# The expert layer in two passes: one rounded matmul per token for the gate spread, first products of all 128 tiles before any second product

## The chip, the cores and the metric

The kernel runs on one core of one Trainium2 chip. The metric is the time of one execution on the device, in microseconds (us). The engines are TensorE (PE; PEld is its loading of weights), VectorE (DVE), ScalarE (ACT), GpSimd (POOL) and SyncE (SP), which here only issues DMAs.

## The reference, cut to what matters

The program is a block of three layers on 256 tokens of width 1024: two attention layers, a mixer with memory attention, and at the end a layer of experts (PEER). Only the expert layer changes:

```python
def _peer(h, w_query, sub_keys, expert_u, expert_v):
    ...
    g = jax.nn.softmax(top_s, axis=-1).astype(h.dtype)
    ...
    def block(args):
        xt, it, gt = args
        u = expert_u[it]
        act = jax.nn.gelu(jnp.einsum('td,tkd->tk', xt, u))
        return jnp.einsum('tk,tkd->td', gt * act, expert_v[it])
```

There are 128 x 128 = 16384 experts. Each token picks 128 (8 heads, 16 each) by two indices of 0 to 127 and has a gate for each pick. The kernel does it densely: gelu(h u) is made for all experts in 128 tiles of 128 experts, multiplied by a matrix W of gates (zero where a token did not pick the expert), and multiplied by v. The output is the residual plus that, normalised.

## The kernel before, in words

**Precision.** A product of float32 factors is made of three matmuls in the rounded type fp32r: each factor is split into a rounded part (hi, made by ACT as a copy into `whi`, `ghi`) and a remainder (lo, made by DVE or POOL by a subtraction into `wlo`, `glo`); hi x hi, hi x lo and lo x hi are summed. So a tile of u or v (128 partitions x 1024 columns, 512 KB) passes through: a DMA into `raw` or `xw`, ACT's copy, the subtraction, then PE.

**First product** of a tile: 8 steps of 128 along the width. Into a bank of 256 tokens go 16 matmuls of 256 columns with hi weights (`hThi`, `hTlo`) and 8 with lo weights. ACT then applies gelu. **Second product** of a tile: for 2 halves of tokens and 2 halves of the output 3 matmuls of 512 columns each, 12 in all; they accumulate over all tiles in banks 0 to 3, which no other work can use from then on.

**W.** For each token one matmul of two one-hot matrices (rows: its 128 picks; `first_hot` scaled by the gates, `second_hot`) gives its 128 x 128 slice of W. It is a full float32 matmul of 128 columns. DVE makes the one-hots for groups of 8 tokens (L2505, two instructions of 1024 columns), POOL (L1373) and ACT (L1732) multiply by the gates, PE does 8 matmuls per group (`w_group`, L1250, two records each in the trace), ACT copies them from PSUM into the arena, four tokens at a time (L1724).

**Order.** (1) NA = 48 tiles have only their first product early (`early_product`, lines 702 and 705), while DVE picks the experts; after gelu their activations go to DRAM (`spill`, L609). The 32 groups of W stand in pairs behind tiles 29 to 44. (2) The first product of two further tiles and their second, as the hand-over. (3) A loop in rounds of six tiles (`expert_loop`, 78 tiles in all): first product of tile j in a wide form (8 matmuls of 512 columns, L1321, that take hThi and hTlo side by side, and 8 of 256, L1324; ACT and DVE add the halves by L1770 and L2523), then second product of tile j - 2 (L1297). Each load brings u and v together, 1024 KB. (4) The tail: second products of the 48 early tiles. SP issues for tile i the 512 KB of v (L648) and right behind it the 128 KB of activations (L652) into one of 32 places of the arena, with at most four on the way; DVE multiplies them by W (`weigh_again`, L2569), ACT rounds (L1822), DVE subtracts (L2581).

Each engine and the SP queue take their instructions in the written order; semaphores (`wait_ge`) tie them together.

Of the kernel before, what the change touches and what calls it, by code (L numbers as in the profile page):

```python
# [29 lines left out]
XRING = 3  # L30
XBODY = 6
NL = 2 + XBODY * 13
NA = N_KEYS - NL
E_AT = (12, 23)
ACT_GATES = 1
SEL0_AT = 19
SEL1_AT = 27
G0 = 29
GROUPS_W = T // 8
G1 = G0 + GROUPS_W // 2  # L40
HEAD = [(NA + 2 * tile + part, tile, part) for tile in range(2) for part in range(2)]
RAW_OF = [i % 4 if i < G0 - 5 else i % 3 for i in range(NA)] + [0, 1, 2, 0]
SPLIT_OF = [i % 4 if i < G0 - 5 else i % 3 for i in range(NA)] + [0, 1, 2, 3]
LAST_OF_FOUR = G0 - 6


def before(ring, i):

    earlier = [j for j in range(i) if ring[j] == ring[i]]
    return earlier[-1] if earlier else None  # L50


def groups_at(i):

    return range(2 * (i - G0), 2 * (i - G0) + 2) if G0 <= i < G1 else range(0)
# [66 lines left out]
def build(nc, x_d, mem_d, keep_d, tab_d, sml_d, frt_d, final_d, w_d, sk_d, ex_d, out_d):  # L122
    ctx = ExitStack()
    with ctx:
# [53 lines left out]
        def fr(name):  # L178
# [46 lines left out]
        uhi_ready, ulo_ready, vhi_ready, vlo_ready, ghi_ready, glo_ready = (  # L225
            sem(n) for n in ("uhi_ready", "ulo_ready", "vhi_ready", "vlo_ready", "ghi_ready", "glo_ready"))
        iota_ready = sem("iota_ready")
        hotA, hotB, hotC, x_kept = sem("hotA"), sem("hotB"), sem("hotC"), sem("x_kept")
        ex_loaded = [sem(f"ex_loaded{i}") for i in range(XRING)]

# [25 lines left out]
        head_half = sem("head_half")  # L256
        hot_ready, wt_done, wt_taken = sem("hot_ready"), sem("wt_done"), sem("wt_taken")
        aex_loaded = [sem(f"aex_loaded{i}") for i in range(4)]
        auhi_ready, aulo_ready, aa_done, aa_gelu = (sem(n) for n in ("auhi_ready", "aulo_ready", "aa_done", "aa_gelu"))
        act_stored = [sem(f"act_stored{i}") for i in range(3)]  # L260
        act_back = [sem(f"act_back{i}") for i in range(4)]
        b_taken, sum_ready = sem("b_taken"), sem("sum_ready")
        a_done, a_gelu, g_ready, v_done = sem("a_done"), sem("a_gelu"), sem("g_ready"), sem("v_done")
# [152 lines left out]
        iota_ps = bank[4][:, 0:P]  # L416
        wbank = bank[6:8]
# [126 lines left out]
        head_bank = [bank[5 + (NA + n - G1) % 3] for n in range(2)]  # L544
        head_first = [q for q in HEAD if q[2] == 0]

        def early_bank(i):

            return bank[6 + i % 2] if i < G0 else bank[5] if i <= G1 else bank[5 + (i - G1) % 3]

        def ex_slot(i):

            return (i - 2) % XRING

        def ex_uses(i):

            return (i - 2) // XRING + 1

        vslots = [w for i in range(4) for w in [(i % 2, D if i >= 2 else 0)]]

        def v_at(i):

            b, at = (i % 2, D) if i < NL else vslots[(i - NL) % 4]
            return b, slice(at, at + D)

        act_again = [arena[:, 14 * T + T * (m % 32):14 * T + T * (m % 32) + T] for m in range(NA)]
# [3 lines left out]
        def _(sp_):  # L570
# [35 lines left out]

            def store_act(i):
                sp_.wait_ge(aa_gelu, i + 1)
                sp_.dma_start(spill[i], staged[i % 3]).then_inc(act_stored[i % 3], 16)  # L609

            for i in range(NA + 4):
                if i < 2:
                    sp_.wait_ge(lo_ready, len(SPLIT_UNITS) - 3)
                elif i < 4:
                    sp_.wait_ge(lo_ready, len(SPLIT_UNITS) - 2)
                else:
                    sp_.wait_ge(aulo_ready, before(RAW_OF, i) + 1)
                if i < NA:
                    rows_of_u = ex_d[NL + i][:, 0:D]
                else:  # L620
                    _, tile, part = HEAD[i - NA]
                    rows_of_u = ex_d[tile][:, D * part:D * part + D]
                sp_.dma_start(aslots[RAW_OF[i]], rows_of_u).then_inc(aex_loaded[RAW_OF[i]], 16)
                if i >= 6:
                    store_act(i - 6)
            for i in range(NA - 2, NA):
                store_act(i)

            for i in range(2, 2 + XRING):
                sp_.wait_ge(aulo_ready, NA + 3 if i == 2 else NA + 4)  # L630
                sp_.wait_ge(wt_done, T // 4)
# [2099 lines left out]
```

## Time and profile before

| | us |
|---|---|
| three runs, median (lowest, highest) | 1509.1 (1508.21, 1510.73) |
| the profiled execution | 1509.89 |
| its span, first to last instruction | 1508.1 |
| PE busy in the span | 1470.0 |
| DVE, ACT, POOL busy | 889.2, 819.0, 576.4 |

Of the profiled execution's time 1.8 us lie outside its span. Busy shares are means over stages with different limits, so they are read stage by stage below.

### The profile page before, as it was taken

The numbers are of one execution on the slowest core, as the hardware profiler recorded it, in microseconds if no ns is written. First come the engines' busy times: TensorE is split into PE (matmuls) and PEld (weight loads), VectorE is DVE, ScalarE is ACT, GpSimd is POOL, SyncE is SP. The second block draws the span as 40 slices with busy tenths as digits, with TensorE's granted clock in tenths as the row PEclk, the third lists the DMA queues.
The fourth block names the chain that finished last, engine by engine and source line by source line (L and its number), as shares of the span: only waits on it lengthen the run. The fifth ranks groups of instructions, "written<-read, shape, count | busy, mean of one in ns | idle before, by whom it ended". The sixth has DMA issues, their size and how long they took to land.

```text
span 1508.1 us, 24377 instructions
## 1 busy us (share of the span) xinstructions
PE 1470.0 (97%) x8923; PEld 1302.1 (86%) x8923; DVE 889.2 (59%) x2185; ACT 819.0 (54%) x1483; POOL 576.4 (38%) x200
## 2 busy tenths in 40 slices
PE   7999999999999999989999999999999999999998
PEld 6788888788889898889999998888888888887886
DVE  4935259388336431225996662666666666667776
ACT  5556454488456644443556664555555555555554
POOL 6881665700467477456888884000000000000000
PEclk9999999999999999999999999999999999999999
DMA  8740435600334335333665334555555555556774
GB/s 332 274 169 29 167 129 177 225 30 2 108 121 163 140 141 183 121 143 113 197 211 153 98 105 161 196 195 194 185 185 189 193 195 195 186 189 219 243 241 163
DMA packets 60125, 251.08 MB, mean 166 GB/s; under 512 B 6144, under 2 KB 18560, under 8 KB 44160
## 3 DMA queue, kind: packets, MB, share of 16 engines
q1 hardware_dynamic: 60032, 249.86, 47.9%
q8 instruction: 56, 0.92, 0.3%
q14 instruction: 37, 0.30, 0.1%
HBM read 242.50 MB, written 7.34 MB: 166 GB/s over the span
## 4 chain that ended last, share of the span: by engine, by line
PE 66%; POOL 2%; ACT 2%; DVE 1%; issue 1%; DMA 0%; DVEq 0%; ACTq 0%
PE bank L1297 23%; PE bank L1321 9%; PE bank L702 6%; PE bank L869 6%; PE bank L1324 5%; PE bank L1250 4%; PE bank L705 3%; POOL wlo L1364 2%; PE bank L822 2%; PE bank L764 1%; PE bank L805 1%; ACT whi L1421 1%; PE bank L724 1%; PE bank L998 1%; PE bank L1150 1%; PE bank L980 1%
## 5 line engine op out<-in xcount | busy, mean ns | idle before, releaser
L1364 POOL TENSOR_TENSOR wlo<-raw,whi 128x2048 fp32r<-128x2048 f32 (+1 forms) x51 | 195.3, 3840 | 159.0 <-ACT whi L1421 158.7
L1364 POOL TENSOR_TENSOR wlo<-arena,whi 128x2048 fp32r<-128x2048 f32 (+1 forms) x45 | 195.1, 4342 | 151.1 <-ACT whi L1421 150.9
L1297 PE MATMUL bank<-whi,ghi 128*128 128x512 f32 x512 | 201.4, 393 | 3.6 <-DVE glo L2559 1.7
L1297 PE MATMUL bank<-wlo,ghi 128*128 128x512 f32 x512 | 201.0, 393 | 0.0
L1297 PE MATMUL bank<-whi,glo 128*128 128x512 f32 x512 | 200.0, 391 | 0.0
L1321 PE MATMUL bank<-hT,whi 128*128 128x512 f32 x624 | 154.3, 390 | 1.6 <-ACT whi L1767 1.6
L1321 PEld LDWEIGHTS bank<-hT,whi 128*128 128x128 f32 x624 | 117.0, 188 | 26.0 <-ACT whi L1767 1.8
L2516 DVE TENSOR_TENSOR wlo<-raw,whi 128x1024 fp32r<-128x1024 f32 x84 | 102.8, 1225 | 56.6 <-ACT whi L1774 56.6
L1377 POOL TENSOR_TENSOR wlo<-raw,whi 128x1024 fp32r<-128x1024 f32 x52 | 123.8, 2391 | 28.2 <-ACT whi L1717 28.1
L1421 ACT ACTIVATE whi<-arena 128x2048 fp32r<-128x2048 f32 x41 | 78.4, 1915 | 94.4 <-PE bank L822 28.7
L822 PE MATMUL bank<-whi,hT 128*128 128x512 f32 x512 | 125.8, 393 | 0.0
L1774 ACT ACTIVATE whi<-raw 128x1024 fp32r<-128x1024 f32 x84 | 88.5, 1055 | 62.9 <-PE bank L1297 59.5
L1421 ACT ACTIVATE whi<-raw 128x2048 fp32r<-128x2048 f32 x39 | 74.7, 1915 | 87.0 <-PE bank L822 40.9
L1297 PEld LDWEIGHTS bank<-whi,ghi 128*128 128x128 f32 x512 | 96.9, 189 | 23.3 <-issue 2.2
L1297 PEld LDWEIGHTS bank<-whi,glo 128*128 128x128 f32 x512 | 96.6, 189 | 20.8
L822 PEld LDWEIGHTS bank<-whi,hT 128*128 128x128 f32 x512 | 95.1, 188 | 19.1
L1297 PEld LDWEIGHTS bank<-wlo,ghi 128*128 128x128 f32 x512 | 96.8, 189 | 17.1
L702 PE MATMUL bank<-hT,whi 128*128 128x256 f32 x800 | 105.8, 285 | 0.0
L702 PEld LDWEIGHTS bank<-hT,whi 128*128 128x128 f32 x800 | 99.3, 192 | 0.5 <-issue 0.5
L1324 PEld LDWEIGHTS bank<-hT,wlo 128*128 128x128 f32 x624 | 85.1, 191 | 6.1
L1777 ACT ACTIVATE ghi<-gact 128x256 fp32r<-128x256 f32 x78 | 32.6, 418 | 105.5 <-DVE gact L2527 105.5
L1324 PE MATMUL bank<-hT,wlo 128*128 128x256 f32 x624 | 87.0, 283 | 0.0
(336 smaller groups left out, 3027.0 us busy)
## 6 DMA issues: line engine op xcount, KB each, us to landing
raw<-ex_in SPq DMA_DIRECT2D x52, 1024.0 KB, 4.8
raw<-w_in SPq DMA_DIRECT2D x44, 1024.0 KB, 5.2
arena<-w_in SPq DMA_DIRECT2D x44, 1024.0 KB, 5.1
raw<-ex_in SPq DMA_DIRECT2D x84, 512.0 KB, 3.9
xw<-ex_in SPq DMA_DIRECT2D x26, 1024.0 KB, 4.7
xw<-ex_in SPq DMA_DIRECT2D x16, 512.0 KB, 4.0
arena<-spill SPq DMA_DIRECT2D x48, 128.0 KB, 3.8
spill<-gact SPq DMA_DIRECT2D x32, 128.0 KB, 3.7
```

Of the source, the lines that this page charges most:

```text
L702: mm(out, lhs, rhs, start=(k == 0), stop=False)
L822: last = mm(out, h[:, KT // 2 * half + k, P * j:P * j + P], w[:, :, k, :], start=(half == 0 and i == 0 and k == 0), stop=(half == 1 and i ...
L869: last = mm(bank[2 * (c % 2) + b][:, T * at:T * at + T], w[:, k, P * j:P * j + P], h[:, k, :], start=first, stop=final)
L1250: last = mm(wbank[h][:, P * j:P * j + P], first[:, 4 * h + j, :], second[:, 4 * h + j, :], start=True, stop=True)
L1297: last = mm(bank[2 * t + h][:, :], g[:, j % 2, tok], w[:, b, at], start=False, stop=(final and i == 2), skip_group_check=True)
L1321: mm(out, lhs, rhs, start=(k == 0), stop=False)
L1324: last = mm(out, lhs, rhs, start=False, stop=(k == KT - 1))
L1364: last = G.tensor_tensor(wlo[:, u % 2, at], slots[u % RING][:, at], whi[:, u % 2, at], ALU.subtract)
L1377: G.tensor_tensor(alo[SPLIT_OF[i]], aslots[RAW_OF[i]], ahi[SPLIT_OF[i]], ALU.subtract).then_inc(aulo_ready, 1)
L1421: A(whi[:, u % 2, :], slots[u % RING], ACT.Copy).then_inc(hi_ready, 1)
L1774: A(whi[:, b, at], xslots[ex_slot(i)][:, D:2 * D], ACT.Copy).then_inc(vhi_ready, 1)
L2516: V.tensor_tensor(wlo[:, b, at], xslots[ex_slot(i)][:, D:2 * D], whi[:, b, at], ALU.subtract).then_inc(vlo_ready, 1)
```

## The change

All 128 tiles get their first product first, in the narrow form of 24 matmuls, and all their activations go to DRAM; then all 128 second products follow, each reading its activations back. There are no rounds and no hand-over. Work is counted in NU = 256 units of 512 KB: unit n < 128 is u of tile n, unit 128 + m is v of tile m. The units pass through a ring of four places (three from unit 24 on: `quarters`, `hi4`, `lo4`). The remainders are made by POOL, by DVE for every third unit from tile 31 on, and by DVE for all units of v (`BY_DVE`).

For W, the gate of a pick is rounded; the rounded value and its remainder stand side by side, so one fp32r matmul of 256 columns per token gives both parts. ACT copies the rounded part of two tokens into W, DVE adds the remainder part (`add_low`). W is now laid out tile after tile in the order of tokens, so both touch single elements that lie 1 KB apart; before, runs of four neighbours were written. A group of 8 tokens is cut into four quarters of two tokens; two quarters stand behind each of two tiles out of three, from tile 31 (`HOT0`) to tile 125. DVE makes the plain one-hot (1024 columns), then half-wise the product with the gates' remainders and the second one-hot (4 instructions of 512); POOL multiplies by the rounded gates (2 of 512).

In the second pass the activations of tile m go into one of three places (`again`, m % 3), by a load that SP issues behind the load of unit m + 129.

```diff
-NL = 2 + XBODY * 13
-NA = N_KEYS - NL
+HOT0 = 31
+NU = 2 * N_KEYS
+RING_OF = [n % 4 if n < G0 - 5 else n % 3 for n in range(NU)]
+BY_DVE = [n >= 2 * N_KEYS - 128 or (n > HOT0 and n % 3 == HOT0 % 3) for n in range(NU)]
...
+def next_in(n):
+    return [j for j in range(n + 1, min(n + 5, NU)) if earlier(j) == n]
...
+def quarters_at(i):
+    g, at = divmod(i - HOT0, 3)
+    return range(4 * g + 2 * at, 4 * g + 2 * at + 2) if 0 <= g < GROUPS_W and at < 2 else range(0)
...
+        gate_lo = xw[:, 3 * T:4 * T]
+        quarters, hi4, lo4 = ([w[:, i // 2, D * (i % 2):D * (i % 2) + D] for i in range(4)] for w in (raw, whi, wlo))
+        plain_hot = quarters[3].rearrange("p (j n) -> p j n", j=8)
+        gated = [w[3].rearrange("p (a j n) -> p a j n", a=2, j=4) for w in (hi4, lo4)]
+        second_hot = [w[:, :, :].rearrange("p a t -> p (a t)").rearrange("p (j n) -> p j n", j=4) for w in (ghi, glo)]
+        staged = [gact[:, 0], gact[:, 1], xw[:, 4 * T:5 * T]]
+        again = [xw[:, T * (5 + i):T * (6 + i)] for i in range(3)]
+        spill = nc.dram_tensor("spill", (N_KEYS, P, T), FP32, kind="Internal").ap()
...
+            def load_act(m):
+                if m >= 3:
+                    sp_.wait_ge(g_ready, m - 2)
+                sp_.wait_ge(act_stored[m % 3], 16 * (m // 3 + 1))
+                sp_.dma_start(again[m % 3], spill[m]).then_inc(act_back[m % 3], 16)
...
+            for n in range(NU):
...
+                    by_dve, by_pool = lows_upto(earlier(n))
+                    if BY_DVE[earlier(n)]:
+                        sp_.wait_ge(u_lo_dve, by_dve)
+                    else:
+                        sp_.wait_ge(u_lo_pool, by_pool)
+                sp_.dma_start(quarters[RING_OF[n]], ex_d[n][:, 0:D] if n < N_KEYS else ex_d[n - N_KEYS][:, D:2 * D])\
+                   .then_inc(u_loaded[RING_OF[n]], 16)
+                if 6 <= n < N_KEYS + 6:
+                    store_act(n - 6)
+                m = n - 1 - N_KEYS
+                if m >= 0:
+                    load_act(m)
+            load_act(N_KEYS - 1)
+            sp_.wait_ge(glo_ready, 16)
...
+            def hot_quarter(k):
+                g, q = divmod(k, 4)
+                pe.wait_ge(hi_gated, g + 1)
+                pe.wait_ge(hots_ready, g + 1)
+                if k >= 2:
+                    pe.wait_ge(w_added, k - 1)
+                for j in range(2):
+                    token = 2 * q + j
+                    last = mm(hot_bank[k % 2][:, T * j:T * j + T].rearrange("p (a n) -> p a n", a=2),
+                              second_hot[token // 4][:, token % 4, :], gated[token // 4][:, :, token % 4, :], start=True, stop=True)
+                last.then_inc(w_done, 1)
+            for i in range(N_KEYS):
+                first_product(i)
+                if i in SEL_AT:
+                    transposes(("sel0", "sel1")[SEL_AT.index(i)])
+                for k in quarters_at(i):
+                    hot_quarter(k)
...
+            def second_ready(m):
+                pe.wait_ge(glo_ready, m + 1)
+                low_ready(N_KEYS + m)
+            for m in range(N_KEYS - 2):
+                second_ready(m)
                 for t in range(TT):
+                    last = out_part(m, t, False)
+                last.then_inc(u_done, 1)
...
+            for n in range(N_KEYS):
+                if not BY_DVE[n]:
+                    pool.wait_ge(u_hi, n + 1)
+                    G.tensor_tensor(lo4[RING_OF[n]], quarters[RING_OF[n]], hi4[RING_OF[n]], ALU.subtract).then_inc(u_lo_pool, 1)
+                g, at = divmod(n - HOT0 + 1, 3)
+                if at == 0 and 0 <= g < GROUPS_W:
+                    pool.wait_ge(plain_ready, g + 1)
+                    for half in range(2):
+                        some = slice(4 * half, 4 * half + 4)
+                        last = G.tensor_tensor(gated[half][:, 0], plain_hot[:, some],
+                                               idx8[:, 2, g, some].unsqueeze(2).to_broadcast([P, 4, P]), ALU.mult)
+                    last.then_inc(hi_gated, 1)
...
+            def act_hi(m):
+                if m < N_KEYS:
+                    act.wait_ge(g_ready, m + 1)
+                    if m >= 2:
+                        act.wait_ge(u_done, N_KEYS + m - 1)
+                    A(ghi[:, m % 2, :], W[:, m, :], ACT.Copy).then_inc(ghi_ready, 1)
+            for n in range(4):
+                unit_hi(n)
+            for n in range(NU - 2):
+                act.wait_ge(u_done, n + 1)
+                if n < N_KEYS:
+                    if n >= 3:
+                        act.wait_ge(act_stored[n % 3], 16 * (n // 3))
+                    A(staged[n % 3], first_bank(n)[:, 0:T], ACT.Gelu_apprx_tanh).then_inc(act_ready, 1)
+                    for k in quarters_at(n):
+                        act.wait_ge(w_done, k + 1)
+                        A(W[:, :, 2 * k:2 * k + 2].rearrange("p n t -> p t n"),
+                          hot_bank[k % 2][:, :].rearrange("p (t a n) -> p t a n", t=2, a=2)[:, :, 0, :],
+                          ACT.Copy).then_inc(w_copied, 1)
+                if n + 2 >= N_KEYS:
+                    act_hi(n + 2 - N_KEYS)
+                for j in next_in(n):
+                    unit_hi(j)
...
+            def plain(g):
+                if g == 0:
+                    dve.wait_ge(u_lo_pool, lows_upto(LAST_OF_FOUR)[1])
+                    dve.wait_ge(u_done, LAST_OF_FOUR + 1)
+                else:
+                    dve.wait_ge(w_done, 4 * g)
+                V.tensor_tensor(plain_hot, iota8, idx8[:, 1, g].unsqueeze(2).to_broadcast([P, 8, P]),
+                                ALU.is_equal).then_inc(plain_ready, 1)
+            def hots(g):
+                dve.wait_ge(plain_ready, g + 1)
+                for half in range(2):
+                    some = slice(4 * half, 4 * half + 4)
+                    V.tensor_tensor(gated[half][:, 1], plain_hot[:, some],
+                                    gate_lo8[:, g, some].unsqueeze(2).to_broadcast([P, 4, P]), ALU.mult)
+                    last = V.tensor_tensor(second_hot[half], iota8[:, 0:4],
+                                           idx8[:, 0, g, some].unsqueeze(2).to_broadcast([P, 4, P]), ALU.is_equal)
+                last.then_inc(hots_ready, 1)
+            def add_low(k):
+                dve.wait_ge(w_copied, k + 1)
+                to = W[:, :, 2 * k:2 * k + 2].rearrange("p n t -> p t n")
+                V.tensor_tensor(to, hot_bank[k % 2][:, :].rearrange("p (t a n) -> p t a n", t=2, a=2)[:, :, 1, :], to,
+                                ALU.add).then_inc(w_added, 1)
+            def weigh(m):
+                if m < N_KEYS:
+                    dve.wait_ge(act_back[m % 3], 16 * (m // 3 + 1))
+                    V.tensor_tensor(W[:, m, :], again[m % 3], W[:, m, :], ALU.mult).then_inc(g_ready, 1)
+            def act_lo(m):
+                if m < N_KEYS:
+                    dve.wait_ge(ghi_ready, m + 1)
+                    V.tensor_tensor(glo[:, m % 2, :], W[:, m, :], ghi[:, m % 2, :], ALU.subtract).then_inc(glo_ready, 1)
+            plain(0)
+            hots(0)
+            for n in range(HOT0 - 3, NU - 2):
+                some = quarters_at(n)
+                if len(some) and some[0] % 4 == 2 and some[0] // 4 + 1 < GROUPS_W:
+                    plain(some[0] // 4 + 1)
+                for k in some:
+                    add_low(k)
+                if len(some) and some[0] % 4 == 2 and some[0] // 4 + 1 < GROUPS_W:
+                    hots(some[0] // 4 + 1)
+                if n == N_KEYS - 2:
+                    dve.wait_ge(w_added, 4 * GROUPS_W)
+                    weigh(0)
+                if n + 2 >= N_KEYS:
+                    act_lo(n + 2 - N_KEYS)
+                if n + 3 >= N_KEYS and n + 3 - N_KEYS >= 1:
+                    weigh(n + 3 - N_KEYS)
+                if n + 3 < NU and BY_DVE[n + 3]:
+                    unit_lo(n + 3)
```

## Rows read from the trace of the kernel before

**Rows 1.** The page: span, and busy time of each engine.
```profile
span 1508.1 us, 24377 instructions
PE 1470.0 (97%) x8923; PEld 1302.1 (86%) x8923; DVE 889.2 (59%) x2185; ACT 819.0 (54%) x1483; POOL 576.4 (38%) x200
```

**Rows 2.** Busy time by stretch, expert layer (the header names the columns).
```profile
core 0: us, PE busy (x) PEld busy (x) DVE busy (x) ACT busy (x) POOL busy (x), PEclk, DMA share, GB/s
808.25:927.70 119.45, 119.45 (x1018) 118.62 (x1016) 72.22 (x63) 75.58 (x138) 103.06 (x54) 1.00 0.36 111
927.70:944.10 16.40, 13.05 (x58) 10.66 (x57) 7.17 (x17) 6.06 (x11) 0.54 (x1) 0.90 0.55 202
944.10:1360.50 416.40, 416.40 (x2117) 355.97 (x2118) 269.50 (x379) 225.04 (x378) 0.00 (x0) 1.00 0.54 190
1360.50:1502.30 141.80, 139.91 (x614) 114.40 (x612) 99.74 (x158) 72.23 (x110) 0.00 (x0) 1.00 0.69 222
```

**Rows 3.** Timeline of PE, last groups and early tiles (start, duration).
```profile
909.56 1.95 PE L1250 MATMUL bank<-whi,raw 128*128 128x128 f32 x16
913.17 2.16 PE L702 MATMUL bank<-hT,whi 128*128 128x256 f32 x16
916.13 2.08 PE L702 MATMUL bank<-hT,whi 128*128 128x256 f32 x16
919.01 2.08 PE L702 MATMUL bank<-hT,whi 128*128 128x256 f32 x16
```

**Rows 4.** Timeline of PE, one pass of the rounds, and its neighbours.
```profile
974.55 0.40 PE L1297 MATMUL bank<-whi,ghi 128*128 128x512 f32 x1
...
977.29 1.98 PE L1321 MATMUL bank<-hT,whi 128*128 128x512 f32 x8
...
980.06 0.40 PE L1297 MATMUL bank<-whi,ghi 128*128 128x512 f32 x1
```

**Rows 5.** Timeline of PE, hand-over to the rounds and to the tail.
```profile
808.25 2.08 PE L702 MATMUL bank<-hT,whi 128*128 128x256 f32 x16
...
944.07 2.14 PE L1321 MATMUL bank<-hT,whi 128*128 128x512 f32 x8 [1.62 <-ACT whi L1767]
...
1367.13 0.47 PE L1297 MATMUL bank<-whi,ghi 128*128 128x512 f32 x1 [1.03 <-DVE glo L2529]
...
1501.98 0.39 PE L1297 MATMUL bank<-whi,glo 128*128 128x512 f32 x1
```

**Rows 6.** Groups by line and shape: busy us, mean ns, idle before.
```profile
L2505 DVE TENSOR_TENSOR raw<-bank,xw 128x1024 f32<-128x1024 f32 x16 | 19.6, 1225 | 29.2 <-PE bank L1250 29.1
L1961 DVE TENSOR_TENSOR hT<-bank,arena 128x512 fp32r<-128x512 f32 x16 | 10.7, 689 | 73.6 <-PE bank L822 25.8 <-PE bank L805 23.9 <-PE bank L694 18.6
L1377 POOL TENSOR_TENSOR wlo<-raw,whi 128x1024 fp32r<-128x1024 f32 x52 | 123.8, 2391 | 28.2 <-ACT whi L1717 28.1
L1373 POOL TENSOR_TENSOR raw<-raw,xw 128x896 f32<-128x896 f32 x16 | 27.0, 1686 | 4.2 <-DVE raw L2505 4.2
L1724 ACT ACTIVATE arena<-bank 128x512 f32<-128x512 f32 x64 | 38.2, 598 | 23.8 <-PE bank L1250 23.8
L1516 ACT ACTIVATE arena<-bank 128x256 f32<-128x256 f32 x64 | 24.0, 375 | 8.2 <-PE bank L987 7.5
L2104 DVE TENSOR_REDUCE arena<-gact 128x64 f32<-128x192 f32 x32 | 11.8, 369 | 0.2
L2099 DVE TENSOR_TENSOR gact<-bank,sc 128x192 f32<-128x192 f32 x32 | 11.4, 357 | 4.7 <-PE bank L998 4.1
```

**Rows 7.** Timeline of DVE, ACT and the SP queue, one tail period.
```profile
1439.65 0.43 DVE L2581 TENSOR_TENSOR glo<-arena,ghi 128x256 fp32r<-128x256 f32 x1 [0.54 <-ACT ghi L1822]
1439.99 0.42 DVE L2569 TENSOR_TENSOR arena<-arena 128x256 f32<-128x256 f32 x1
...
1440.60 1.23 DVE L2516 TENSOR_TENSOR wlo<-raw,whi 128x1024 fp32r<-128x1024 f32 x1 [0.19 <-ACT whi L1774]
...
1441.85 0.33 SPq L648 DMA_DIRECT2D raw<-ex_in  x1
...
1442.23 0.43 SPq L652 DMA_DIRECT2D arena<-spill  x1
1442.25 1.04 ACT L1774 ACTIVATE whi<-xw 128x1024 fp32r<-128x1024 f32 x1
...
1442.37 0.43 DVE L2581 TENSOR_TENSOR glo<-arena,ghi 128x256 fp32r<-128x256 f32 x1 [0.54 <-ACT ghi L1822]
```

**Rows 8.** Activations read back (L652), starts 1366.1 to 1404.1.
```profile
DMA to landing us min/median/max: 3.2/4.6/5.5
```

**Rows 9.** The same for starts 1406.9 to 1434.1 (11 of them).
```profile
DMA to landing us min/median/max: 3.1/3.6/3.8
```

**Rows 10.** The same for starts 1436.8 to 1486.0 (19 of them).
```profile
DMA to landing us min/median/max: 3.2/3.9/5.3
```

More of the change, by code:

```diff
@@ L255, in build @@
         half_done, half_out = sem("half_done"), sem("half_out")
[L256 to L263, printed above, removed]
+        wt_taken = sem("wt_taken")
         out_ready, out_stored = sem("out_ready"), sem("out_stored")
@@ L542, in build, with first_bank @@
         ysq = arena[:, 3 * D:3 * D + CW]
[L544 to L566, printed above, removed]
+        def first_bank(i):
+            return bank[6 + i % 2] if i < G0 else bank[5 + (i - G0) % 2]
+        W = arena[:, :].rearrange("p (n t) -> p n t", t=T)
         @block.sync
@@ L605, in _ @@
                 load(u)
+            def load_act(m):
[3 more added lines that the diff above has]
+                sp_.dma_start(again[m % 3], spill[m]).then_inc(act_back[m % 3], 16)
             def store_act(i):
-                sp_.wait_ge(aa_gelu, i + 1)
+                sp_.wait_ge(act_ready, i + 1)
                 sp_.dma_start(spill[i], staged[i % 3]).then_inc(act_stored[i % 3], 16)
[L611 to L615, printed above, removed]
-                else:
[L617 to L625, printed above, removed]
@@ L1275, in _ @@
-            for n, (i, tile, part) in enumerate(head_first):
-                pe.wait_ge(auhi_ready, i + 1)
-                pe.wait_ge(aa_gelu, NA - 2 + n)
-                h, l = (w[SPLIT_OF[i]].rearrange("p (k n) -> p k n", k=KT) for w in (ahi, alo))
-                products(head_bank[n][:, 0:T], [(h[:, k, :], t[:, k, :]) for k in range(KT) for t in (hThi, hTlo)],
-                         [(l[:, k, :], hThi[:, k, :]) for k in range(KT)],
-                         lambda: pe.wait_ge(aulo_ready, i + 1)).then_inc(a_done, 1)
@@ new lines, in first_product @@
+                out = first_bank(i)[:, 0:T]
+                for k in range(KT):
+                    for r, rows_of_k in enumerate((hThi, hTlo)):
+                        mm(out, h[:, k, :], rows_of_k[:, k, :], start=(k == 0 and r == 0), stop=False)
+                low_ready(i)
+                for k in range(KT):
+                    last = mm(out, l[:, k, :], hThi[:, k, :], start=False, stop=(k == KT - 1))
+                last.then_inc(u_done, 1)
[10 more added lines that the diff above has]
+                last.then_inc(w_done, 1)
@@ L1293, in out_part @@
+            for i in range(N_KEYS):
[4 more added lines that the diff above has]
+                    hot_quarter(k)
+            def out_part(m, t, final, columns=range(2)):
+                n = N_KEYS + m
                 for h in columns:
-                    at = slice(half.start + CW * h, half.start + CW * h + CW)
+                    at = slice(CW * h, CW * h + CW)
@@ L2550, in _ @@
-            dve.wait_ge(a_gelu, 2)
-            dve.wait_ge(wt_taken, T // 8 + 8)
-            for n in range(2):
-                last = V.tensor_tensor(gact[:, n, 0:P], gact[:, n, 0:P], Wg[:, T * n:T * n + P], ALU.mult)
-            step(last)
-            for n in range(2):
-                last = V.tensor_copy(ghi[:, n, 0:P], gact[:, n, 0:P])
-            step(last)
-            for n in range(2):
-                V.tensor_tensor(glo[:, n, 0:P], gact[:, n, 0:P], ghi[:, n, 0:P], ALU.subtract).then_inc(head_half, 1)
```

378 lines of the change are left out of this document (59 added, 319 removed).

## Prediction, made before the changed kernel ran

> **What bounds the kernel now.** The page first [rows 1]: PE is busy 1470 of 1508 us, every other engine under 60%. The stretches next [rows 2]: in the expert layer, from 808 us on, PE is busy to the full except in the 16.4 us of the hand-over to the rounds, where 3.35 us are idle and the granted clock falls to 0.90, and 1.9 us around the start of the tail. So a change pays here by taking time from PE, or costs by making PE wait. For a new wait I read the period of the tail [rows 7] and the landings of its loads [rows 8 to 10]; the tail is what the second pass will look like.
>
> **PE's work, part by part.** W: from 909.56 to 913.17 PE does two groups, 16 tokens, in 3.61 us, and the tile behind them takes 2.96 us where the one after takes 2.88 [rows 3]. That is 3.69 us a pair, 59.0 us for 16 pairs. The new matmul has 256 columns of fp32r, the shape of a first product's: 24 of them take 2.88 us [rows 3], 0.12 us each. 256 tokens cost 30.7 us: 28.3 us saved.
>
> First products: 78 tiles leave the wide form, 977.29 to 980.06 = 2.77 us [rows 4], for 2.88 us: 78 x 0.11 = 8.6 us lost.
>
> Hand-overs: between the end of tile 47 (the last of four pitches of 2.88 from 916.13, so 927.65) and 944.07 [rows 3, 5] PE does two second products (2.72 us each) and two wide first ones (2.77), 11.0 us of work in 16.4: 5.4 us go. At the tail's start 1.9 us go [rows 2], and a second product takes 2.74 us in the rounds [rows 4] and 2.72 in the tail (1439.65 to 1442.37, paced by PE [rows 7]): 1.6 us.
>
> Check by one count: from tile 29's start at 808.25 to the last product's end at 1502.3 [rows 5] are 694.0 us; the new order needs 99 x 2.88 + 30.7 + 128 x 2.72 = 664.0. I take 29.5 us saved if PE never waits.
>
> **First pass: does PE wait?** The work for a group of W has three tiles and eight tokens of PE time, 9.6 us. DVE: 1.23 for the plain one-hot, 4 x 0.69 for the halves, 4 x 0.42 for the additions (as the 256-column L2581 [rows 7]), 1.23 for one remainder [rows 6]: 6.9 us. ACT: three copies of 1.04, three gelus and four copies from PSUM of 0.38 [rows 6, 7]: 5.8. POOL: two remainders of 2.39, and two products of 512 columns at 1.686 x 512/896 = 0.96 [rows 6]: 6.7. All fit. The order is tightest on DVE: a group's plain one-hot can only start when the last quarter before it is done, and its first matmul comes two tiles, 5.76 us, later. DVE does in between 1.23 + 2 x 0.42 + 4 x 0.69 = 4.8 us; POOL's products are ready at 1.3 + 1.9 = 3.2 us, its next remainder at 5.6, wanted at 5.76 + 0.48 + 1.92 = 8.2. Margin 0.9 us. Behind POOL's delayed remainder stand SP's load and store, and so one gelu in three comes some 0.7 us late; two banks cover it. No wait: 0 us.
>
> What no row shows is a write of single elements 1 KB apart. From below: no cost, since DVE reads 192 elements 256 bytes apart in 369 ns, against 357 for 192 in order, and ACT reads PSUM 512 bytes apart at 598 ns for 512 [rows 6]. From above: POOL's rate of 2.33 ns an element [rows 6], 0.6 us for 256; then DVE needs 5.2 us of the 5.76, and PE still does not wait. Only above 0.9 us an addition does PE stall. I take the row's value, no cost.
>
> The Trainium skill (SBUF — State Buffer, Door 1: The DMA port swizzle) says that consecutive accesses within a 16-byte line run at full rate and each step to a new line pays a penalty, which speaks against this layout; L2104 shows no such penalty for DVE's reads, and no row here shows the writes.
>
> **Second pass: a ring around the activations.** Before, SP read the activations four tiles ahead. Now load_act(m) stands behind the load of unit m + 129, which waits until DVE has made the remainder of unit m + 126, and DVE makes that right behind weigh(m - 2). weigh(m) waits for the landing, and its loop holds back the next remainder. So two tiles take one turn of this circle: weigh to remainder 0.34 (pitch of two 256-column instructions, 1439.65 to 1439.99), remainder 1.23, SP's issue of the unit 0.02 behind its end, of the activations 0.38 behind that (1441.85 to 1442.23) [rows 7], landing L, and some 0.05 to start DVE. T = (2.02 + L)/2 per tile; PE needs 2.72. They are equal at L = 3.42.
>
> L in the tail has medians of 4.6, 3.6 and 3.9 us, minimum 3.1 [rows 8 to 10]. The first belongs to loads that were issued faster than PE's pace (16 in 38.0 us); the second is the steady state. There a pair lands 3.6 + 0.38 = 4.0 us after its first issue while the next pair starts at 2.72, so pairs overlap; a longer T overlaps less. I take L = 3.65: T = 2.835.
>
> The start: units 126 and 127 free their places early, load_act(2) waits for the remainder of unit 128, which DVE ends near the end of the last-but-one first product. Counted from that end, weigh(2) starts at about 0.2 + 0.4 + 3.9 = 4.5 us. After weigh(m) come the remainder (to 1.6 us) and the activation's remainder (0.43): product m starts 2.05 us later at the earliest. Product 127 then starts at 4.5 + 2.05 + 125 T = 6.55 + 354.4 = 360.9, and by PE's own work at 2.88 + 127 x 2.72 = 348.3. Stall 12.6 us, rounded up to 13.5 for landings that scatter, since one late landing delays two tiles and is not made up.
>
> **Sum.** -29.5 + 13.5 = -16 us: a span of 1492. The profiled execution took 1.8 us more than its span, and the runs' median lies 0.8 us below it: 1509.1 - 16 = 1493 us.
>
> The Trainium skill (DMA: Bandwidth & Descriptors, Latency and other measured facts) says that the fixed part of a transfer shrinks when HBM is less loaded; by it L falls as T grows and the stall is nearer to its lower end; rows 9 against rows 8 agree.
>
> **Rivals.** (a) PE never waits: L under 3.42, or the circle is broken by some slack that I don't see. Time 1509.1 - 29.5 = 1479.6. For it: minimum landings of 3.1; against: no median is below 3.6. Chance 0.20. (b) My forecast, stall of 5 to 24 us, 1485 to 1504: 0.52. (c) The other side: the circle runs with the tail's worse landings. At L = 3.96, T = 2.99 and the stall, 6.55 + 373.8 - 348.3 = 32, eats all; at 4.2, T = 3.11 gives 47 us and 1526. Slower from L = 4.0 on. For it: medians of 3.9 and 4.6; against: those stretches hold pairs issued closer together than the circle allows. Chance 0.14, half of it beyond 1512. (d) The first pass stalls, by strided writes or another order than mine on DVE: at 1.15 us an addition, 2 x (1.15 - 0.9) = 0.5 us a group, 16 us over 32, with (b) 1509. Chance 0.09. The line rule of the Trainium skill (SBUF — State Buffer, Door 1: The DMA port swizzle) would be such a case. (e) The new matmul costs more than 0.12 us, as weights and columns change with each token: at the old token's 0.114 x 2 = 0.228 nothing of W's 28 us is saved; with (b) about 1520. Chance 0.05.
>
> **Numbers.** A difference of 0.2%, 3 us, is what a measurement can tell. Faster: (a), (b) and a fifth of the rest, 0.78; within 3 us: 0.09; slower: 0.13. The range from 1479 to 1512 holds all of (a) and (b) and half of the others; the likeliest case's own is 1485 to 1504.
>
> **What the profile after would show.** PE's hot products at a pitch of 0.12 us, tiles at 2.88, groups at 9.6; no clock of 0.5 between the passes. In the second pass DVE waits for a DMA from `spill` before `weigh`, PE for `glo`, and tiles lie 2.8 to 2.9 us apart, from about product 15 on; by (a) 2.72 with no such wait; by (c) 3.0 or more. ACT's copies into W take 0.38 us and DVE's additions 0.42; longer ones speak for (d). The forecast is wrong if landings are not those of the tail, if the circle has a link that I missed, or if quarters make PE wait.

## The result, and the profile after

The changed kernel takes 1733.65 us (median of 4 runs, 1732.01 to 1734.17), the kernel before on the same chip 1509.91 (4 runs, 1508.21 to 1513.26). The ratio is 1.1477, with a 95% interval of 1.1455 to 1.1499. The forecast was 1493, with a range to 1512 and 0.78 on faster: wrong in sign, and by 241 us.

The page of the changed kernel, for [rows 1]: the span, busy time of each engine, and the span in 40 slices (PEclk is the granted clock in tenths).

```profile
span 1731.5 us, 25221 instructions
PE 1544.2 (89%) x9291; PEld 1371.0 (79%) x9291; DVE 1094.2 (63%) x2283; ACT 817.3 (47%) x1437; POOL 719.7 (42%) x276
PE   8999999999999998999767767767767999999997
PEclk9999999999999999999878788888888999999999
```

PE has a hole in slices 20 to 31, where the clock falls too. The windows cut there, for [rows 2]: from the layer's first product to the first group of W, from there to the last group, and the rest.

```profile
core 0: us, PE busy (x) PEld busy (x) DVE busy (x) ACT busy (x) POOL busy (x), PEclk, DMA share, GB/s
727.90:821.80 93.90, 93.40 (x776) 92.96 (x775) 84.13 (x300) 49.36 (x70) 79.89 (x35) 1.00 0.67 208
821.80:1341.60 519.80, 380.74 (x2561) 374.98 (x2560) 402.80 (x320) 195.82 (x321) 239.15 (x126) 0.82 0.41 124
1341.60:1725.40 383.80, 369.68 (x1539) 281.74 (x1537) 242.21 (x388) 177.37 (x263) 0.00 (x0) 1.00 0.69 216
```

The account. The middle stretch has 96 tiles and 256 tokens, reckoned at 96 x 2.88 + 30.7 = 307.2 us. It took 519.8, 212.6 more: 139.1 in which PE is idle (519.80 - 380.74), and 73.5 in which it does the same work slower (380.74 - 307.2), at a granted clock of 0.82. The second pass took 383.8 for 348.2: 35.6 more. The layer starts 4.2 us later than before (727.9 against 723.70). With the 29.5 us that the forecast saves on PE's work that makes 212.6 + 35.6 + 4.2 - 29.5 = 222.9; the spans differ by 223.4.

What PE waited for in the layer (waits of the changed kernel: engine, line, releaser; us in total, times, longest):

```profile
PE bank L1223 <- issue: 137.6, 31, 4.9
DVE arena L2377 <- DMA xw<-spill: 138.4, 119, 2.8
PEld bank L1240 <- DVE glo L2383: 44.5, 82, 2.0
```

The first product of each group of W waits 4.4 us, 31 times. The profile puts it down to "issue", so the cause has to be read from what ends just before. PE around one group:

```profile
1013.10 1.12 PE L1211 MATMUL bank<-hT,wlo 128*128 128x256 f32 x8
1018.64 1.20 PE L1223 MATMUL bank<-whi,ghi 128*128 128x256 f32 x4 [4.42 <-issue]
1019.64 3.57 PE L1208 MATMUL bank<-hT,whi 128*128 128x256 f32 x16
1023.05 1.11 PE L1211 MATMUL bank<-hT,wlo 128*128 128x256 f32 x8
1024.00 0.64 PE L1223 MATMUL bank<-wlo,glo 128*128 128x256 f32 x4
```

PE is ready at 1014.22 and starts at 1018.64. Behind the wait 16 matmuls take 3.57 us, where they took 2.08 [rows 3]. Behind the wait before this one, also of 4.4 us, they took 2.87. Windows over the two stretches behind the wait show the granted clock (the third column from the end):

```profile
1018.60:1023.10 4.50, 4.46 (x21) 4.49 (x22) 2.73 (x3) 2.14 (x3) 0.00 (x0) 0.51 0.39 136
...
1023.10:1026.00 2.90, 2.90 (x26) 2.90 (x26) 1.32 (x2) 1.80 (x4) 0.02 (x1) 1.00 0.67 190
```

In the wait itself (1014.2 to 1018.6) the mean is 0.73, so the clock falls there, while PE does nothing. 0.51 is the lower of the two levels, 1.2 GHz; after 4.5 us of work it is back at 2.4 GHz. The second four products of W, at 1024.00, lie in 0.47 us, 0.12 each as forecast. DVE and POOL in the same window (timeline of the changed kernel):

```profile
1008.50 1.23 DVE L2352 TENSOR_TENSOR raw<-keep,xw 128x1024 f32<-128x1024 f32 x1 [1.16 <-PE bank L1223]
...
1009.64 1.41 DVE L2370 TENSOR_TENSOR arena<-bank,arena 128x256 f32<-128x256 f32 x2
1009.81 1.04 POOL L1294 TENSOR_TENSOR whi<-raw,xw 128x512 fp32r<-128x512 f32 x1 [7.90 <-DVE raw L2352]
...
1010.81 1.04 POOL L1294 TENSOR_TENSOR wlo<-raw,xw 128x512 fp32r<-128x512 f32 x1
1010.97 1.43 DVE L2360 TENSOR_TENSOR whi<-raw,xw 128x512 fp32r<-128x512 f32 x1
...
1011.81 5.58 POOL L1288 TENSOR_TENSOR wlo<-raw,whi 128x1024 fp32r<-128x1024 f32 x2
1012.32 2.87 DVE L2362 TENSOR_TENSOR ghi<-keep,xw 128x512 fp32r<-128x512 f32 x1
...
1015.12 2.82 DVE L2360 TENSOR_TENSOR wlo<-raw,xw 128x512 fp32r<-128x512 f32 x1
...
1017.86 0.68 DVE L2362 TENSOR_TENSOR glo<-keep,xw 128x512 fp32r<-128x512 f32 x1
```

The four half-wise instructions of DVE, priced at 0.69 us each, take 1.43, 2.87, 2.82 and 0.68. The short one is the one beside which POOL does nothing. The first ends 0.55 us behind the end of a POOL instruction (1012.40 against 1011.85), the third 0.55 behind the end of POOL's pair of remainders (1017.94 against 1017.39): each looks like an instruction of some 0.6 us that began when POOL's ended. PE starts 0.1 us behind the fourth. The groups of the changed kernel give it for all 32 (busy us, mean ns), to be set against [rows 6]:

```profile
L2360 DVE TENSOR_TENSOR whi<-raw,xw 128x512 fp32r<-128x512 f32 x32 | 44.5, 1389 | 0.0
L2362 DVE TENSOR_TENSOR ghi<-keep,xw 128x512 fp32r<-128x512 f32 x32 | 90.6, 2831 | 0.0
L2360 DVE TENSOR_TENSOR wlo<-raw,xw 128x512 fp32r<-128x512 f32 x32 | 89.0, 2781 | 0.0
L2362 DVE TENSOR_TENSOR glo<-keep,xw 128x512 fp32r<-128x512 f32 x32 | 23.9, 746 | 0.0
L2370 DVE TENSOR_TENSOR arena<-bank,arena 128x256 f32<-128x256 f32 x128 | 94.0, 782 | 54.0 <-ACT arena L1655 54.0
L1655 ACT ACTIVATE arena<-bank 128x256 f32<-128x256 f32 x128 | 76.9, 705 | 147.7 <-PE bank L1223 147.7
L1288 POOL TENSOR_TENSOR wlo<-raw,whi 128x1024 fp32r<-128x1024 f32 x96 | 255.3, 2679 | 24.5 <-ACT whi L1635 24.3
```

The four together take 7.75 us a group where 2.76 were reckoned. 0.68 us is the usual time of the fourth; its mean of 746 ns holds one case, in the first group, where it lay beside POOL and took 2.9. The same rows show a second surprise: writes into W take 782 and 705 ns where 420 and 375 were reckoned. What differs in the operands: before, the number row that the one-hots compare with was read from PSUM (`iota_ps`, in bank 4); the change needs bank 4 for W's products and reads the row from SBUF (`keep`), and its remainders of the gates too (`gate_lo` in `xw`). So both operands of all four lie in SBUF.

### The profile page after: what moved, and what is told of

Read it like the earlier page. It is cut to its first block, busy times and chain, and to the rows that moved or that the text cites. A ratio compares the mean times of both kernels' runs of the same rounds, so it can differ in the third digit from the quotient of the medians.

```text
span 1731.5 us, 25221 instructions
## 1 busy us (share of the span) xinstructions
PE 1544.2 (89%) x9291; PEld 1371.0 (79%) x9291; DVE 1094.2 (63%) x2283; ACT 817.3 (47%) x1437; POOL 719.7 (42%) x276
## 3 DMA queue, kind: packets, MB, share of 16 engines
q8 instruction: 74, 1.21, 0.3%
## 4 chain that ended last, share of the span: by engine, by line
PE 40%; DMA 14%; issue 9%; DVE 7%; POOL 2%; ACT 1%; SPq 1%; DVEq 0%; ACTq 0%
PE bank L1208 16%; DMA xw<-spill 14%; PE bank L1211 7%; PE bank L824 5%; DVE wlo L2336 4%; PE bank L1223 3%; POOL wlo L1281 2%; PE bank L777 2%; DVE arena L2377 2%; SPq L610 1%; PE bank L719 1%; PE bank L760 1%; ACT whi L1338 1%; PE bank L953 1%; PE bank L1105 1%
## 5 line engine op out<-in xcount | busy, mean ns | idle before, releaser
L1208 PE MATMUL bank<-hT,whi 128*128 128x256 f32 x2048 | 309.7, 312 | 0.0
L1208 PEld LDWEIGHTS bank<-hT,whi 128*128 128x128 f32 x2048 | 298.5, 222 | 0.5 <-issue 0.5
L1635 ACT ACTIVATE whi<-raw 128x1024 fp32r<-128x1024 f32 x256 | 274.8, 1074 | 3.6 <-DMA raw<-ex_in 3.6
L1288 POOL TENSOR_TENSOR wlo<-raw,whi 128x1024 fp32r<-128x1024 f32 x96 | 255.3, 2679 | 24.5 <-ACT whi L1635 24.3
L2336 DVE TENSOR_TENSOR wlo<-raw,whi 128x1024 fp32r<-128x1024 f32 x160 | 195.2, 1220 | 0.5 <-ACT whi L1635 0.2
L1223 PE MATMUL bank<-whi,ghi 128*128 128x256 f32 x128 | 37.5, 443 | 137.6 <-issue 137.6
L1211 PE MATMUL bank<-hT,wlo 128*128 128x256 f32 x1024 | 154.6, 297 | 0.5 <-POOL wlo L1288 0.5
L1655 ACT ACTIVATE arena<-bank 128x256 f32<-128x256 f32 x128 | 76.9, 705 | 147.7 <-PE bank L1223 147.7
L1211 PEld LDWEIGHTS bank<-hT,wlo 128*128 128x128 f32 x1024 | 144.9, 209 | 0.7 <-POOL wlo L1288 0.7
L2377 DVE TENSOR_TENSOR arena<-xw,arena 128x256 f32<-128x256 f32 x128 | 54.4, 425 | 138.6 <-DMA xw<-spill 138.4
L2370 DVE TENSOR_TENSOR arena<-bank,arena 128x256 f32<-128x256 f32 x128 | 94.0, 782 | 54.0 <-ACT arena L1655 54.0
```

Source lines behind the costliest of these rows:

```text
L1208: mm(out, h[:, k, :], rows_of_k[:, k, :], start=(k == 0 and r == 0), stop=False)
L1211: last = mm(out, l[:, k, :], hThi[:, k, :], start=False, stop=(k == KT - 1))
L1223: last = mm(hot_bank[k % 2][:, T * j:T * j + T].rearrange("p (a n) -> p a n", a=2), second_hot[token // 4][:, token % 4, :], gated[token / ...
L1288: G.tensor_tensor(lo4[RING_OF[n]], quarters[RING_OF[n]], hi4[RING_OF[n]], ALU.subtract).then_inc(u_lo_pool, 1)
L1635: A(hi4[RING_OF[n]], quarters[RING_OF[n]], ACT.Copy).then_inc(u_hi, 1)
L2336: V.tensor_tensor(lo4[RING_OF[n]], quarters[RING_OF[n]], hi4[RING_OF[n]], ALU.subtract).then_inc(u_lo_dve, 1)
```

## The experiments

Two theories at the outset, for the first pass. **Operands**: a DVE instruction with both operands in SBUF waits for POOL's running instruction; then one operand in PSUM, or a short POOL instruction, cures it. **Writes**: the scattered writes into W hold DVE back (rival (d)); then writing in runs cures it. A third, that these instructions are slow by themselves, whatever POOL does, is tested by b_pool_short. For the second pass: the **circle** of the prediction against mere slow landings or too few places. Runs given with one time were executed once.

**a_psum: one operand of each of DVE's one-hot instructions in PSUM.** Bank 3 is free until the second pass; the matmul that brought the last quarter of the residual there moves behind the first pass. Its operand stays in `xw` until then, so the three places of the activations move to other parts of `xw`.

```diff
-        gate_lo = xw[:, 3 * T:4 * T]
+        gate_lo = bank[3][:, T:2 * T]
...
-            iota8 = tb("iota", KEEP, keep).unsqueeze(1).to_broadcast([P, 8, P])
+            iota_ps = bank[3][:, 0:P]
+            step(V.tensor_copy(iota_ps, tb("iota", KEEP, keep)))
+            iota8 = iota_ps.unsqueeze(1).to_broadcast([P, 8, P])
...
```

> Theory P (a DVE instruction with two operands in SBUF and a POOL instruction do not run together: one waits for the other's end): with the number row and the gate remainders in a PSUM bank the four half-wise instructions of a group fall from 7.8 us in sum to 4 x 0.69 = 2.8 us although POOL works as before; the first quarter of a group no longer waits 4.4 us, the clock stays at its upper level, a group's period falls from 16.4 to 9.6-10.2 us, and the span from 1731.5 to about 1525 us (31 x 6.5 us less). Rival S (single elements 1 KB apart in W set the pace, 705 ns for ACT's copy and 782 ns for DVE's addition): these are unchanged here, so the period stays above 14 us.

1526.71 us, 207 less than the changed kernel. Its groups:

```profile
L2363 DVE TENSOR_TENSOR whi<-raw,bank 128x512 fp32r<-128x512 f32 x32 | 21.9, 686 | 0.0
L2365 DVE TENSOR_TENSOR ghi<-bank,xw 128x512 fp32r<-128x512 f32 x32 | 22.0, 688 | 0.0
L2373 DVE TENSOR_TENSOR arena<-bank,arena 128x256 f32<-128x256 f32 x128 | 99.6, 826 | 63.2 <-ACT arena L1656 63.0
L1289 POOL TENSOR_TENSOR wlo<-raw,whi 128x1024 fp32r<-128x1024 f32 x96 | 230.2, 2419 | 26.4 <-ACT whi L1636 26.1
L1223 PE MATMUL bank<-whi,ghi 128*128 128x256 f32 x128 | 21.2, 288 | 1.8 <-issue 1.5
```

The half-wise instructions take 0.69 us, as priced, though POOL works beside them; PE's wait falls from 137.6 us to 1.5, and the clock is back at 0.996. The writes are as slow as before (826 ns), so they did not cause the wait. At that length DVE's way to a group's first matmul just fits: the forecast had let PE stall only above 0.9 us an addition. POOL gains too: 2419 ns for 2679.

**b_pool_short: the operands stay in SBUF, POOL is short.** Behind unit 31 POOL's remainders cover only 64 of 1024 columns; the other 960 are left out.

```diff
-                    G.tensor_tensor(lo4[RING_OF[n]], quarters[RING_OF[n]], hi4[RING_OF[n]], ALU.subtract).then_inc(u_lo_pool, 1)
+                    some = slice(0, D if n <= HOT0 else 64)
+                    G.tensor_tensor(lo4[RING_OF[n]][:, some], quarters[RING_OF[n]][:, some], hi4[RING_OF[n]][:, some],
+                                    ALU.subtract).then_inc(u_lo_pool, 1)
```

> POOL's remainders behind unit 31 are made for 64 of 1024 columns only (the rest of these remainders is left as it was, so part of the computation is left out); all DVE operands stay in SBUF. Theory P: the four half-wise DVE instructions take about 0.69 us each but for those that meet POOL's two products of 1.05 us, 3 to 4.5 us in sum, period about 10 to 11 us, span about 1540. Rival Q (these instructions are slow by themselves, because both operands are read from SBUF, one of them broadcast): they stay at 1.4, 2.8, 2.8 and 0.7 us, period 16.4 us.

1538.39 us. The two half-wise instructions that lay beside POOL's remainders fall; the first, beside POOL's gate products, which are unchanged, does not:

```profile
L2362 DVE TENSOR_TENSOR whi<-raw,xw 128x512 fp32r<-128x512 f32 x32 | 44.0, 1375 | 0.0
L2364 DVE TENSOR_TENSOR ghi<-keep,xw 128x512 fp32r<-128x512 f32 x32 | 26.6, 830 | 0.0
L2362 DVE TENSOR_TENSOR wlo<-raw,xw 128x512 fp32r<-128x512 f32 x32 | 26.4, 825 | 0.0
```

So it is POOL's instruction beside them that costs, by its length, and not the operands alone: with POOL idle the changed kernel's fourth instruction took 0.68 us with both operands in SBUF, as against 0.69 with one in PSUM.

**a2_iota: only the number row in PSUM**, so that the two one-hots of L2365 have one operand there, and the two products of L2363 both still in SBUF. The matmul and the places of the activations move as in a_psum.

```diff
-            iota8 = tb("iota", KEEP, keep).unsqueeze(1).to_broadcast([P, 8, P])
+            iota_ps = bank[3][:, 0:P]
+            step(V.tensor_copy(iota_ps, tb("iota", KEEP, keep)))
+            iota8 = iota_ps.unsqueeze(1).to_broadcast([P, 8, P])
...
```

> Only the number row goes to PSUM; the remainders of the gates stay in SBUF, so of the four half-wise instructions the two second one-hots have one operand in SBUF and the two products two. Theory P, by instruction: the one-hots take 0.69 us, the products still wait for POOL's running instruction, 1.4-2.8 us each; sum about 5.5 us, the first quarter is late by 1-3 us, period 11-13 us, span between 1570 and 1640. Theory by stage (once POOL is less in the way everything clears): near a_psum's 1524.9.

1580.55 us. In one kernel, side by side:

```profile
L2363 DVE TENSOR_TENSOR wlo<-raw,xw 128x512 fp32r<-128x512 f32 x32 | 71.4, 2232 | 0.0
L2363 DVE TENSOR_TENSOR whi<-raw,xw 128x512 fp32r<-128x512 f32 x32 | 44.7, 1396 | 0.0
L2365 DVE TENSOR_TENSOR ghi<-bank,xw 128x512 fp32r<-128x512 f32 x32 | 21.7, 677 | 0.0
L1223 PE MATMUL bank<-whi,ghi 128*128 128x256 f32 x128 | 22.7, 299 | 52.4 <-issue 52.4
```

PE waits 31 times here too, but 1.7 us each for 4.4, and the run's clock stays at 0.996: this run pays for little but the waits.

**h_before_sbuf: the kernel before, with its number row read from SBUF.** Nothing of the change is in it.

```diff
-            iota8 = iota_ps.unsqueeze(1).to_broadcast([P, 8, P])
+            iota8 = tb("iota", KEEP, keep).unsqueeze(1).to_broadcast([P, 8, P])
```

> The kernel before, with the number row read from SBUF instead of a PSUM bank, so that its one-hots (two a group, 1024 columns) have both operands in SBUF while POOL multiplies and subtracts. Theory P: the one-hots lengthen from 1.22 us to 1.2-3.5 us, by 1 us on average, a pair of groups needs 4 x 2.2 = 9 us of DVE where 6.56 us were its period, 16 pairs x 2-3 us = 30-50 us more, and POOL's products lengthen too. Rival Q (slow by the form of the instruction, not by POOL): also longer, but equally for all of them; no change at all would speak against both.

1559.0 us, 49 more than the kernel before beside it (1509.66). Its DVE and its POOL, two timelines of one stretch:

```profile
853.67 2.68 DVE L2505 TENSOR_TENSOR raw<-keep,xw 128x1024 f32<-128x1024 f32 x1
856.27 3.40 DVE L2505 TENSOR_TENSOR whi<-keep,xw 128x1024 fp32r<-128x1024 f32 x1
```

```profile
852.67 2.60 POOL L1373 TENSOR_TENSOR xw<-xw 128x896 f32<-128x896 f32 x1 [1.16 <-DVE xw L2505]
855.23 3.36 POOL L1377 TENSOR_TENSOR wlo<-raw,whi 128x1024 fp32r<-128x1024 f32 x1
```

They take turns. In the same stretch the DVE instruction just before, begun at 852.51 while POOL did nothing, took 1.21 us. POOL's product ends at 855.27 and DVE's instruction 1.08 us later, at 856.35; POOL's next one, begun at 855.23, then runs to 858.59, and DVE's again ends 1.08 us behind it. In [rows 6] the same lines took 1225 ns (DVE), 1686 and 2391 (POOL): POOL is held up as well. The clock is at 0.998, so none of the 49 us comes from there.

**c_runs2: W written in runs of two tokens**, the rival's cure.

```diff
-                        A(W[:, :, 2 * k:2 * k + 2].rearrange("p n t -> p t n"),
+                        A(W[:, :, 2 * k:2 * k + 2],
...
-                to = W[:, :, 2 * k:2 * k + 2].rearrange("p n t -> p t n")
+                to = W[:, :, 2 * k:2 * k + 2]
...
```

> The same elements of W are written with the two tokens innermost: runs of two neighbours, 8 bytes, instead of one, and PSUM is read 1 KB apart. If the 1 KB steps of the writes are what made ACT's copy 705 ns (expected 375) and DVE's addition 782 ns (expected 420), they fall to about 0.4-0.55 us each. Theory P: the span moves little, by the 2 x 0.3 us that stand ahead of the half-wise instructions in each group, 31 x 0.6 = 19 us at most, to about 1712-1725. Rival S: the period falls by far more.

1724.06 us.

```profile
L2370 DVE TENSOR_TENSOR arena<-bank,arena 128x256 f32<-128x256 f32 x128 | 55.7, 460 | 49.9 <-ACT arena L1655 48.6
PE bank L1223 <- issue: 132.8, 31, 5.1
```

The writes are cured (ACT 433 ns for 705, DVE 460 for 782), the wait is not: 132.8 us for 137.6. The writes are a true cost and not the cause. The edit also changes the order in which PSUM is read, from neighbours to steps of 1 KB, so the gain is that of both together.

**d_deep and f_one_earlier: the second pass alone.** d_deep gives the activations six places for three and asks for them two units earlier; f_one_earlier keeps the three places and asks one unit earlier.

```diff
-                m = n - 1 - N_KEYS
-                if m >= 0:
+                m = n + 1 - N_KEYS
+                if 0 <= m < N_KEYS:
...
```

```diff
-                m = n - 1 - N_KEYS
+                m = n - N_KEYS
...
```

> Activations come back through six places instead of three and are asked for two units earlier (load_act(m) behind unit m + 127). Theory of the circle (weigh, remainder, issue, landing, two tiles a turn): DVE no longer waits 138 us for these loads, PE's 14 us idle and 35 us of stretched second pass go, second pass from 383.7 to about 350 us, span about 1697. Rival (DMA throughput bounds the second pass): it stays near 380 us, the wait moves to the loads of the units.

> Three places as in the changed kernel, only the load of activations m stands behind unit m + 128 instead of m + 129. The circle then takes three tiles a turn, (1.97 + 3.9)/3 = 1.96 us a tile, under PE's 2.72: as with six places, DVE's 138 us of waits and 35 us of the second pass go, span near 1697. Rival (six places were what helped, not the order): span near 1731.

1698.33 and 1697.98 us: spans of 1696.5 and 1696.2, 35.0 and 35.3 less than 1731.5, which is the 35.6 us of the account. In both DVE's wait for `spill` is gone and the wait for W's groups stays (136 us). The number of places was not to blame, the place of `load_act` in SP's order was. Nor were the landings by themselves: their medians are 4.3 and 4.4 us in these two runs, longer than the changed kernel's 3.8, and DVE waits for none. They cost only where the circle holds them.

**e_all, g_small, i_no_runs: the repairs together.** e_all has a_psum's operands, runs of two, five places and loads two units earlier. g_small has three places and one unit earlier. i_no_runs is e_all without the runs of two.

> The three repairs together: number row and gate remainders in PSUM (residual of the last quarter of the output added after the first pass), W written in runs of two, activations back through five places and two units earlier. If the parts are what the single runs say: 1524.9 (first repair alone) less 35 us (second pass without its circle) less 1 to 4 us (31 groups whose first quarter comes 0.1-0.2 us late on DVE) = 1486-1490 us of span, 1.2-1.5% under the kernel before. Rival: the faster first pass brings a new wait (ACT already waits 98 us for its stores in the first repair's run), and the span stays over 1500.

> As all three repairs, with three places instead of five and one unit earlier instead of two: the same span as with five within 2 us, if three tiles a turn are enough; more if scattered landings (up to 5.5 us) then reach PE.

> All three repairs but the runs of two in W: ACT's copy and DVE's addition stay at 0.76 and 0.82 us. If DVE's way to the first quarter is 1.23 + 1.5 + 4 x 0.60 + 0.35 = 5.5-5.8 us against 5.76, each group is 0.1-0.2 us late: 1482.8 + 3 to 6 = 1486-1489 us of span. If single elements cost nothing where another engine is the bound, 1483.

e_all takes 1484.27 us (median of 5, 1483.58 to 1484.66), the kernel before beside it 1509.66 (9 runs): ratio 0.9829, interval 0.9816 to 0.9843. It is 1.7% faster than the kernel before, and its span, 1482.8 us, lies 3 us under what was expected. g_small, in one run, 1486.51. i_no_runs 1489.79 (4 runs) against 1510.87: ratio 0.9858 [0.9841, 0.9874]; here the writes take 771 and 829 ns for 439 and 472. Its profiled execution is 6.1 us longer than that of e_all, but 1.8 of them lie ahead of the layer; from the first group of W to the second pass it takes 312.7 us for 308.5. So the scattered writes cost some 4 us, about 0.3%. The windows of e_all (they begin 3.8 us ahead of the first group), and of its waits PE's:

```profile
815.00:1126.00 311.00, 310.50 (x2587) 310.28 (x2586) 211.03 (x318) 165.86 (x323) 217.83 (x128) 1.00 0.68 207
1126.00:1474.90 348.90, 348.53 (x1540) 288.09 (x1539) 253.39 (x385) 177.53 (x262) 0.00 (x0) 1.00 0.76 238
```

```profile
PE bank L1224 <- DVE arena L2374: 0.5, 1, 0.5
PE bank L1242 <- DVE glo L2387: 0.4, 1, 0.4
```

## Why the prediction was wrong

**The step that failed: "First pass: does PE wait? ... No wait: 0 us".** Its order on DVE was right: a group's plain one-hot, two additions and four halves have to end within 5.76 us, or PE waits. Its price of the halves, 0.69 us, was not. That is the time of L1961 [rows 6], which has one operand in PSUM, as L2505, the one-hots before, had; the change moves that operand to SBUF, and I did not ask what an operand's place costs. With 7.75 us for 2.76, and 0.36 more for each of two additions, DVE does not fit. From the start of the plain one-hot to the end of the halves it takes 10.04 us (1008.50 to 1018.54), and PE waits 4.4. Shown by a_psum, which changes the operands' place, by b_pool_short, which changes POOL alone, and by h_before_sbuf, without the change around it.

The Trainium skill (SBUF — State Buffer, Who interferes with whom) has this rule: a DVE instruction with two inputs in SBUF contends with a GpSimd instruction that reads SBUF, one fully waiting for the other, and a DVE instruction with at most one such input does not. The traces agree on both halves, 2831 ns against 688. The rule speaks against this change: two of the four halves lie beside POOL's remainders of 2.39 us each [rows 6], and to wait for one of them is already more than the margin of 0.9 us that the prediction had.

**Its price grew by the clock.** Of 212.6 us in the first pass 73.5 are not waiting but slow work behind the waits. No step of mine had a price for that; [rows 2] had shown the clock at 0.90 where PE idled 3.35 of 16.4 us.

**Rival (d), 0.09, had the place of the stall, and neither its mechanism nor its size.** It made the first pass stall by scattered writes, 0.5 us a group. The group grew by (519.8 - 307.2)/31 = 6.9 us, of which 4.4 are waiting. Scattered writes do cost: I priced them by the reads of L2104, which say nothing of writes. They took 1.9 times as long as reckoned on both engines. The line rule of the Trainium skill (SBUF — State Buffer, Door 1: The DMA port swizzle), weighed in the prediction, pointed that way, and runs of two (433 and 460 ns) agree with it. Alone the scattered writes are worth 4 us where PE does not wait (i_no_runs) and some 10 where it does (c_runs2, one run), not 241.

**Second pass: the circle right, its size too small.** DVE waits for `spill`, two tiles at a time, as told (timeline of the changed kernel's DVE):

```profile
1605.15 0.42 DVE L2377 TENSOR_TENSOR arena<-xw,arena 128x256 f32<-128x256 f32 x1 [2.13 <-DMA xw<-spill]
...
1606.96 0.42 DVE L2377 TENSOR_TENSOR arena<-xw,arena 128x256 f32<-128x256 f32 x1
...
1610.94 0.42 DVE L2377 TENSOR_TENSOR arena<-xw,arena 128x256 f32<-128x256 f32 x1 [2.09 <-DMA xw<-spill]
```

Two tiles take 5.79 us here, 2.90 each, as forecast, and the median pitch of the 125 products in the trace is 2.87. But 21 of the pitches are over 3.1 us, and the mean is 2.98. Over the pass the stall was 35.6 us where 13.5 were forecast, as large as rival (c) had it, 32. The mis-sized term is L = 3.65, with the 0.9 us allowed for landings that scatter:

```profile
DMA to landing us min/median/max: 3.4/3.8/5.5
```

I took L between medians, but each late landing holds the circle up and nothing makes it up, so the mean counts: over the 128 landings of the trace it is 3.95 us. SP's issue of the activations came 0.46 us behind the end of the remainder, for 0.40. With these two the forecast's own formula gives T = (2.08 + 3.95)/2 = 3.01 and a stall of 6.55 + 125 x 3.01 - 348.3 = 34.5 us. The rows held it: the 46 landings of [rows 8 to 10] have a mean of 4.07, and only the 11 of [rows 9], which I called the steady state, have 3.5. I had also argued that landings shorten as the pace drops. Against the tail before they did not: 216 GB/s for 222, and a median between those of [rows 9] and [rows 10]. In e_all, at 238 GB/s, the median is 4.2, but the order of its loads differs too, so no run here shows what the pace alone does.

**What held.** PE's sum. e_all, which keeps the change's order and takes the waits away, has a span of 1482.8, where 1508.1 - 29.5 = 1478.6 were counted. Most of the 4.2 us left are found: 1.9 lie ahead of the layer, whose first product starts at 725.62 for 723.70; and the two passes take 308.5 us for 307.2 and 349.4 for 348.2, with PE's waits of 0.9 in them. Rival (e) is refuted: 0.12 us per matmul. The layer starts 1.7 to 4.2 us later in every kernel with the new code. Three of them start it latest, at 727.4 to 727.9 (the changed kernel, d_deep, i_no_runs), and their profiles show a clock of 0.98 from 0 to 100 us, 200 to 300 and 300 to 400, where the kernel before and e_all have 1.00; that goes with some 2 us of it. Where the other 2 come from stays open; no run was made for it.

## What to carry to other kernels

Before DVE and POOL work side by side, write down for each DVE instruction where both operands lie; one that moves out of PSUM to free a bank can cost more than the bank brings, and the operand may find room in a bank that is idle for now. A price taken from a row holds only for the same places of its operands and the same neighbours. A load asked for behind another wait on its queue is late by that wait; here asking one unit earlier with three places gave as much as six places and two units. Where a late landing is not made up, price the circle by the mean of the landings, not by their median.

## What the runs showed of the hardware

- A DVE instruction with both operands in SBUF and one of POOL took turns, each waiting for the other's end: of 512 columns it took 2831 ns on average beside POOL's remainders (changed kernel), 678 with POOL idle, and 688 beside POOL with one operand in PSUM (a_psum). POOL loses too: 1024 columns took 2679 ns on average for 2419, and 896 columns 2665 for 1686 in h_before_sbuf.
- Writes of single elements 1 KB apart: 705 to 771 ns for 256 on ACT, 782 to 829 on DVE; in runs of two 433 and 460. Other instructions of 256 columns that write in order took 375 (L1516 [rows 6]) and 420 (L2581 [rows 7]).
- An idle stretch of 4.4 us in PE cost more than itself: 16 matmuls behind two of them took 2.87 and 3.57 us for 2.08, and over the first pass 139.1 us of idle time came with 73.5 us of slower work. In a2_iota 31 waits of 1.7 us left the clock at 0.996.
- Landings of the 128 KB loads in the changed kernel's second pass: median 3.8 us, mean 3.95, up to 5.5.
